# Log decay of a gated linear attention summed by a DVE scan instead of a TensorE matmul, and the heads' squares halved on GpSimd before their norm

## What is computed

```python
    log_a = jax.nn.log_sigmoid((a_code @ w_alpha + b_alpha).astype(jnp.float32)) / GLA_GATE_TEMP
...
        b = jnp.cumsum(ai, axis=2)                                  # (B,H,C,dk) cumulative log decay
...
        o_inter = jnp.einsum('bhik,bhkv->bhiv', qi * jnp.exp(b), state)
...
        new_state = jnp.exp(b_last[:, :, 0, :])[..., None] * state + jnp.einsum('bhjk,bhjv->bhkv', k_dec, vi)
...
    o = rmsnorm(o.transpose(0, 2, 1, 3), gla_head_norm)             # per-head norm, (B,S,H,dv)
    o = o.reshape(B, S, GLA_VW) * jax.nn.silu(r)
```

## Time and profile before

| what | value |
|---|---|
| median of three runs | 3164.24 us (3163.45 to 3164.89) |
| the profiled execution's own time | 3164.13 us |
| its span on the slowest core (3) | 3162.3 us |
| spans of the eight cores | 3154.3 to 3162.3 us |
| mean granted TensorE clock of the cores | 0.995 to 0.997 |
| PE busy | 3101.8 us, 98% of the span |
| DVE busy | 1186.6 us, 38% |
| ACT busy | 950.2 us, 30% |
| POOL busy | 481.1 us, 15% |

### The profile page before, as it was taken

How to read it: one execution, slowest core, us unless ns; L and a number is a source line. 1 busy time by engine, 2 the same in 40 slices (tenths; PEclk the granted TensorE clock), 3 DMA queues, 4 the chain that set the end, 5 groups by cost and what they waited for, 6 DMA issues and landing times.

```text
span 3162.3 us, 43137 instructions; the slowest of 8 cores (3154.3 to 3162.3 us)
## 1 busy us (share of the span) xinstructions
PE 3101.8 (98%) x15350; PEld 1448.9 (46%) x15350; DVE 1186.6 (38%) x1880; ACT 950.2 (30%) x1637; POOL 481.1 (15%) x557
## 2 busy tenths in 40 slices
PE   6999999999999999999999999999999999999998
PEld 2444454444444454444444445444444444544443
DVE  2231743621421373551332156363232226536212
ACT  3121442521211253252121135243212114425211
POOL 0002111220200220112110112012121021112002
PEclk9999999999999999999999999999999999999999
DMA  8597444335663534334384365232548345422534
GB/s 165 87 162 120 83 81 120 59 62 95 124 122 70 99 68 94 107 67 76 65 170 76 56 107 100 48 120 54 91 92 159 64 79 93 81 67 52 93 67 104
DMA packets 56784, 292.32 MB, mean 92 GB/s; under 512 B 5632, under 2 KB 11136, under 8 KB 32256
## 3 DMA queue, kind: packets, MB, share of 16 engines
q0 software_dynamic: 39024, 251.35, 44.5%
q1 hardware_dynamic: 17552, 38.21, 3.7%
HBM read 495.78 MB, written 22.02 MB: 164 GB/s over the span
## 4 chain that ended last, share of the span: by engine, by line
PE 94%; DVE 2%; DMA 2%; issue 1%; ACT 0%; SPq 0%; DVEq 0%; ACTq 0%; POOLq 0%; POOL 0%
PE psum_all L106 94%; DMA vo_s<-ov_mst 1%; PE psum_all L122 1%; DVE sb_hT L418 1%; DMA sb_small<-small 0%; DVE ov_nmx L1019 0%; DMA sb_slot<-ffn_w 0%; SPq L134 0%; DVE ov_Pm L1031 0%; DVE ov_pwA L733 0%; ACT ov_rstd L412 0%; DVE sb_xT L418 0%; ACT ov_rstd L410 0%; DVE ov_kT L700 0%; DVE ov_pwB L733 0%
## 5 line engine op out<-in xcount | busy, mean ns | idle before, releaser
L106 PE MATMUL psum_all<-sb_hT,sb_slot 128*128 128x512 bf16 x7680 | 1692.4, 380 | 9.0 <-DVE sb_hT L418 7.9
L106 PEld LDWEIGHTS psum_all<-sb_hT,sb_slot 128*128 128x128 bf16 x7680 | 749.8, 98 | 911.6 <-issue 23.9
L106 PE MATMUL psum_all<-ov_gated,sb_slot 128*128 128x512 bf16 x2816 | 613.2, 380 | 3.4 <-DMA sb_slot<-ffn_w 3.4
L518 DVE TENSOR_TENSOR ov_gated<-psum_all,ov_sl 128x512 bf16<-128x512 f32 x352 | 243.4, 692 | 924.0 <-PE psum_all L106 892.9
L515 ACT ACTIVATE ov_sl<-psum_all 128x512 bf16<-128x512 f32 x352 | 210.2, 597 | 902.8 <-PE psum_all L106 870.4
L106 PEld LDWEIGHTS psum_all<-ov_gated,sb_slot 128*128 128x128 bf16 x2816 | 276.0, 98 | 337.1 <-issue 6.1
L387 ACT ACTIVATE ov_sqt<-sb_xT 128x512 bf16<-128x512 f32 x224 | 140.1, 629 | 550.7 <-DVE sb_xT L539 215.8
L394 POOL TENSOR_TENSOR ov_acc<-ov_acc,ov_sqt 128x512 f32<-128x512 f32 x180 | 211.4, 1175 | 482.9 <-ACT ov_sqt L387 480.3
L134 POOL DMA_DIRECT2D sb_slot<-ffn_w x176 | 95.1, 542 | 1238.5 <-PE psum_all L106 1213.6
L106 PE MATMUL psum_all<-sb_slot,sb_hT 128*128 128x512 bf16 x1024 | 235.4, 379 | 2.6 <-DVE ov_kT L700 2.6
L418 DVE SCALAR_TENSOR_TENSOR sb_hT<-sb_xT,sb_small,ov_rstd 128x512 bf16<-128x512 f32 x192 | 141.7, 798 | 29.6 <-ACT ov_rstd L412 29.6
(11 more groups left out here) (138 smaller groups left out, 2007.7 us busy)
## 6 DMA issues: line engine op xcount, KB each, us to landing
sb_slot<-ffn_w POOLq DMA_DIRECT2D x88, 1024.0 KB, 11.2
sb_slot<-ffn_w POOLq DMA_DIRECT2D x88, 704.0 KB, 7.2
sb_slot<-w_in POOLq DMA_DIRECT2D x40, 1024.0 KB, 13.2
out<-sb_xT SPq DMA_DIRECT2D x14, 1024.0 KB, 11.9
ov_xin<-x SPq DMA_DIRECT2D x12, 1024.0 KB, 13.7
sb_slot<-w_up_a POOLq DMA_DIRECT2D x8, 1024.0 KB, 12.5
sb_slot<-w_mix_out POOLq DMA_DIRECT2D x8, 1024.0 KB, 11.2
sb_slot<-kq_s POOLq DMA_DIRECT2D x8, 1024.0 KB, 5.1
```

The costliest lines, as they stand in the source:

```text
L106: ("ins", (lambda e, o=o, l=l, r=r, st=st, sp=sp: e.matmul(o, l, r, start=st, stop=sp)), i == n - 1)
L518: S.op("dve", lambda e, b3=b3, slt=slt, j=j, s=s: e.tensor_tensor(out=gated[:, j, sl(s)], in0=b3[:], in1=slt[:], op=ALU.mult), [bb3, slb[0 ...
```

## The change

`A1` swaps the operands of its matmul, so that channels come out on partitions and tokens along the free dimension (four matmuls of 128 columns instead of one of 512), and its Ln is written back into `zb` in f32. The triangle matmul of `A2` goes; a DVE scan with multiply and add takes its place, 512 elements long, with a mask `segm` that is 0 at each head's first token. It writes `cum`, from which ACT makes `eb` and `enb`. `A2` is split: the scan and the two exponentials stand at the front of the step, ahead of `A1`, and the two multiplications (`A2b`) stand where `A2` stood. A GpSimd addition behind `osq` makes `osm`, the sum of a head's two halves, so `B_norm` needs one matmul instead of two, and `B_norm` stands behind the first filler of the step instead of at its front.

```diff
+    segm = sb("segm", [128, 4, 128], BF16)
...
-    lp2 = [ov(f"lp{i}", 75 + i, [128, 512], BF16) for i in range(2)]
+    cum, cum_b = ov("cum", 75, [128, 512], F32)
...
+    osm, osm_b = ov("osm", 99, [128, 4, 128], BF16)
...
+    S.op("dve", lambda e: e.memset(segm[:], 1.0), [], [cb2])
+    S.op("dve", lambda e: e.memset(segm[:, :, 0:1], 0.0), [], [cb2])
     S.op("dve", lambda e: e.memset(onesD[:], 1.0 / 1024.0), [], [cb2])
...
-            S.mm([(bz[:], aT[:, c * 128:(c + 1) * 128], walpha[:], True, True)], [aT_b[c // 4], wa_b], [bzb])
+            S.mm([(bz[:, h * 128:(h + 1) * 128], walpha[:, h * 128:(h + 1) * 128], aT[:, c * 128:(c + 1) * 128], True, True)
+                  for h in range(4)], [aT_b[c // 4], wa_b], [bzb])
             S.op("act", lambda e: e.activation(out=zb[:], in_=bz[:], func=AF.Exp, scale=-1.0), [bzb], zb_b)
-            S.op("act", lambda e: e.activation(out=lp[:], in_=zb[:], func=AF.Ln, bias=1.0), zb_b, lp_b)
+            S.op("act", lambda e: e.activation(out=zb[:], in_=zb[:], func=AF.Ln, bias=1.0), [], zb_b)
 
         def A2(c):
...
-            bc, bcb = psum()
-            S.mm([(bc[:, h * 128:(h + 1) * 128], lp[:, h * 128:(h + 1) * 128], triB[:], True, True) for h in range(4)],
-                 lp_b + CB, [bcb])
-            S.op("act", lambda e: e.activation(out=eb[:], in_=v4(bc[:]), func=AF.Exp, scale=-1.0 / 16.0), [bcb], eb_b)
-            S.op("act", lambda e: e.activation(out=enb[:], in_=v4(bc[:]), func=AF.Exp, scale=1.0 / 16.0), [bcb], enb_b)
+            S.op("dve", lambda e: e.tensor_tensor_scan(
+                out=cum[:], data0=segm[:].rearrange("p a b -> p (a b)"), data1=zb[:], initial=0.0,
+                op0=ALU.mult, op1=ALU.add), zb_b + CB, cum_b)
+            S.op("act", lambda e: e.activation(out=eb[:], in_=v4(cum[:]), func=AF.Exp, scale=-1.0 / 16.0), cum_b, eb_b)
+            S.op("act", lambda e: e.activation(out=enb[:], in_=v4(cum[:]), func=AF.Exp, scale=1.0 / 16.0), cum_b, enb_b)
+
+        def A2b(c):
...
             S.op("act", lambda e: e.activation(out=osq[:], in_=ov_, func=AF.Square), bank_b[0:2], osq_b)
+            oq = osq[:].rearrange("p (h v) i -> p h v i", v=2)
+            S.op("pool", lambda e: e.tensor_tensor(out=osm[:], in0=oq[:, :, 0, :], in1=oq[:, :, 1, :], op=ALU.add),
+                 osq_b, osm_b)
...
-            oq = osq[:].rearrange("p (h v) i -> p h v i", v=2)
-            S.mm([(v4(bn[:]), onesV[:], oq[:, :, vc, :], vc == 0, vc == 1) for vc in range(2)], osq_b + CB, [bnb])
+            S.mm([(v4(bn[:]), onesV[:], osm[:], True, True)], osm_b + CB, [bnb])
...
         for i in range(12):
             heavy = 3 <= i <= 8
-            if 0 <= i - 4 < 8:
-                B_norm(i - 4)
+            if 0 <= i - 1 < 8:
+                A2(i - 1)
             if i < 8:
                 A1(i)
             fill()
+            if 0 <= i - 4 < 8:
+                B_norm(i - 4)
             if 0 <= i - 1 < 8:
-                A2(i - 1)
+                A2b(i - 1)
             fill()
```

More of the change, by code:

```diff
@@ L769, in A1 @@
             zb, zb_b = zb2[c % 2]
-            lp, lp_b = lp2[c % 2]
             bz, bzb = psum()
-            S.mm([(bz[:], aT[:, c * 128:(c + 1) * 128], walpha[:], True, True)], [aT_b[c // 4], wa_b], [bzb])
+            S.mm([(bz[:, h * 128:(h + 1) * 128], walpha[:, h * 128:(h + 1) * 128], aT[:, c * 128:(c + 1) * 128], True, True)
+                  for h in range(4)], [aT_b[c // 4], wa_b], [bzb])
             S.op("act", lambda e: e.activation(out=zb[:], in_=bz[:], func=AF.Exp, scale=-1.0), [bzb], zb_b)
-            S.op("act", lambda e: e.activation(out=lp[:], in_=zb[:], func=AF.Ln, bias=1.0), zb_b, lp_b)
+            S.op("act", lambda e: e.activation(out=zb[:], in_=zb[:], func=AF.Ln, bias=1.0), [], zb_b)
         def A2(c):
-            lp, lp_b = lp2[c % 2]
+            zb, zb_b = zb2[c % 2]
             eb, eb_b = eb2[c % 2]
@@ L780, in A2 @@
             tk = slice(c * 128, (c + 1) * 128)
-            bc, bcb = psum()
-            S.mm([(bc[:, h * 128:(h + 1) * 128], lp[:, h * 128:(h + 1) * 128], triB[:], True, True) for h in range(4)],
-                 lp_b + CB, [bcb])
-            S.op("act", lambda e: e.activation(out=eb[:], in_=v4(bc[:]), func=AF.Exp, scale=-1.0 / 16.0), [bcb], eb_b)
-            S.op("act", lambda e: e.activation(out=enb[:], in_=v4(bc[:]), func=AF.Exp, scale=1.0 / 16.0), [bcb], enb_b)
+            S.op("dve", lambda e: e.tensor_tensor_scan(
[4 more added lines that the diff above has]
+        def A2b(c):
+            eb, eb_b = eb2[c % 2]
+            enb, enb_b = enb2[c % 2]
+            tk = slice(c * 128, (c + 1) * 128)
             S.op("dve", lambda e: e.tensor_tensor(out=qT[:, :, tk], in0=qT[:, :, tk], in1=eb[:], op=ALU.mult),
```

## The result

The changed kernel is slower: 3294.6 us against 3164.9, a ratio of 1.0408 (95% interval 1.0392 to 1.0425), so 130 us more. The prediction said 3289, in a range of 3240 to 3325.

What follows compares the result with a forecast made beforehand. PE, busy 98%, bounds the kernel before; after the change a step becomes DVE's and ACT's. Per tile 11.5 + 13.6 + 6.0 = 31.1 us, four 124.4; 3164.1 + 124.4 + 0.6 = 3289 us, range 3240 to 3325.

Steps and rivals of the forecast that it cites:

- What the prediction said would show: Scan about 1.2 us, 2.5 beside `Sbf`; DVE idle 4.2; scan to scan 12.9; PE waits some 30 us a tile.
- What is taken off PE: Triangle's four matmuls and one norm matmul go: 0.43 us a chunk, 32 chunks, 13.8 us gained if PE stayed the bound.
- The scan's price: DVE scan of 512 elements taken at 1.2 us, 0.7 kept for the range.
- The order: Seven ACT instructions stand between DVE's scan and its norm multiplications; DVE stands still 4.2 us for them.
- The meeting with `Sbf`: Scan on DVE meets GpSimd's state copy and is stretched: 1.3 us charged, 0 as the other bound.
- (a): Steps 1 to 4: four scans and DVE's waits make PE late, +11.5 us a tile.
- The clock: Lower granted clock behind PE's pauses, 31 us more if uncovered, 3320; part of the heavier rival, chance 0.15.
- the ring: DVE's scan, ACT's instructions, DVE's norm and followers, then the next scan: 12.9 us a step against PE's 9.1.
- (b): Steps 5 to 8: four rings of 12.9 us are 51.6, before 38.0; +13.6 us a tile.
- (c): Steps 9 to 11: no scan, but late addition and norm lie open, +2.5, +2.6 and +0.9, +6.0 us a tile.
- The mask's memset: Once at the start, it stands ahead of the constants the first matmul waits for: 0.6 us.
- The rival on the other side: PE stays the bound because other work covers DVE's stand between scan and norm: 3151 us, chance 0.09.

Runs made afterwards that it cites:

- l_scanalone: Kernel before with only `A1`'s operands swapped and the scan where the triangle matmul stood, no GpSimd addition, norm at the front: 3198.3 to 3199.7 us, ratio 1.012.
- g_cheap: Changed kernel with the scan replaced in its place by an ordinary two-input DVE multiplication: 3281.3 and 3282.7 us, ratio 1.037.
- c_expslate: Changed kernel with ACT's two exponentials moved behind the norm's two instructions: 3252.8 and 3256.7 us, ratio 1.029; the ring left over GpSimd 11.9 to 12.1 us.
- d_tri: Changed kernel with the triangle matmul back instead of the scan, new order and GpSimd addition kept: 3214.7 and 3217.7 us, ratio 1.017.
- j_sbfnext: Changed kernel with GpSimd's state copy `Sbf` issued in the next step, behind the copy of `eb`'s last column: 3257.2 and 3257.8 us, ratio 1.030.
- e_sbflate: Changed kernel with ACT's exponentials behind the norm's instructions and `Sbf` behind the GpSimd addition: 3194.3 to 3199.1 us, ratio 1.010.
- b_noosm: Changed kernel with the GpSimd addition undone, the norm having two matmuls again, order kept: 3283.0 and 3283.7 us, ratio 1.038.

## Why the prediction was right, and where it was off

**What the prediction said would show** did. Outside the four recurrences nothing moved: from the first merge matmul of one tile to the first code matmul (`sb_wa`) of the next it is 641.2 to 641.5 us, before 641.2 to 641.7. PE's waits in a recurrence are 25 to 28 us a tile, where some 30 were foretold and 0.9 stood before.

**What is taken off PE** was right in count: 64 matmuls fewer, at 0.217 us each 13.8 us, and none of it seen in the time.

**The scan's price.** Taken 1.2, with 0.7 as the other bound: 1.22, and 1.21 in all 32 of l_scanalone. The half throughput that the Trainium skill (DVE: opcode table, instruction layouts, handler registers and perf-mode slots, section Datapath and trigger behaviour) gives the scan agrees with the trace: 0.68 for the two-input multiplication in the same place (g_cheap), 1.21 for the scan, 1.8 times as long. That the scan costs as much as the reduction over 1,024 came out as assumed; no run shows that it does so for the reason given.

**The order.** Seven ACT instructions between scan and norm, 4.2 us: 4.24 to 4.37 in steps 4 to 7. That the order on ACT makes this wait is shown by c_expslate, which gives 40 of the 130 us back. It is not the whole loss: without the scan the new order and the addition still lose 52 (d_tri).

**The meeting with `Sbf`.** Charged 1.3: 2.52 - 1.22 = 1.30, and j_sbfnext takes it away. The Trainium skill (SBUF — State Buffer, section SBUF: two separate sides) has one instruction hold the shared ports as a whole. The trace agrees here as well: the scan ends 1.1 us behind `Sbf`, nearly its own length of 1.22. That GpSimd's addition is stretched by the scan in turn (2.06 for 1.15) was not in my sum; it costs nothing beside the longer ring, but is in c_expslate's 12.1.

**(a) Steps 1 to 4: the term that was mis-sized**, 11.5 a tile. From the code's matmuls to the start of step 5, PE took 1144.23 - 1111.84 = 32.4 us before and 1193.33 - 1146.45 = 46.9 after: 14.5. The rows that bound the stretches, before and after:

```profile
1111.84 0.61 PE L106 MATMUL psum_all<-sb_hT,sb_wa 128*32 128x512 bf16 x8
1214.38 1.89 PE L106 MATMUL psum_all<-ov_ogT,sb_slot 128*128 128x512 bf16 x8
...
1146.45 0.62 PE L106 MATMUL psum_all<-sb_hT,sb_wa 128*32 128x512 bf16 x8
1193.33 0.39 PE L106 MATMUL psum_all<-ov_aT,sb_walpha 128*128 128x128 bf16 x4
1243.07 3.62 PE L106 MATMUL psum_all<-sb_hT,sb_slot 128*128 128x512 bf16 x16
1281.24 1.89 PE L106 MATMUL psum_all<-ov_ogT,sb_slot 128*128 128x512 bf16 x8
```

DVE, whose rows the sum had followed, shows what the missing 3.0 us are:

```profile
1157.36 0.69 DVE L589 TENSOR_SCALAR ov_vtok<-psum_all 128x512 bf16<-128x512 f32 x1 [0.92 <-ACT ov_vtok L587]
...
1177.05 0.69 DVE L704 CAST ov_kT<-psum_all 128x512 bf16<-128x512 f32 x1 [3.23 <-PE psum_all L106]
...
1193.67 0.69 DVE L589 TENSOR_SCALAR ov_vtok<-psum_all 128x512 bf16<-128x512 f32 x1 [1.03 <-PE psum_all L106]
```

In step 1, DVE's v eviction waits 0.92 us for ACT's, because both write the same buffer mark, and ACT's is behind `eb`. The key eviction behind the banks comes 3.23 us late, where the sum had 2.6. And ahead of step 5's scan DVE waits 1.03 us for PE. The rest, 0.4 us, is in the scans and in the waits for `eb` and `rsn`. The 1.03 us comes from PE's lower clock behind its second long pause:

```profile
1163.28 5.89 PE L106 MATMUL psum_all<-sb_hT,sb_slot 128*128 128x512 bf16 x16 [4.41 <-ACT ov_zb L777]
...
1184.63 0.38 PE L106 MATMUL psum_all<-ov_vtok,ov_kg 128*128 128x256 bf16 x2 [3.77 <-ACT ov_zb L777]
...
1186.33 3.57 PE L106 MATMUL psum_all<-sb_slot,sb_hT 128*128 128x512 bf16 x8
```

Behind the first pause, 4.41 us and not 3.3, 16 matmuls took 5.89 us instead of 3.62 at a granted clock of 0.60, and by the rows it cost nothing: neither DVE nor ACT waited for them, and PE itself then waited again for `zb`. The clock was one of my rivals, at 31 us if nothing covered it. It fell as that rival said, but most of what it took is inside the ring's slack; e_sbflate and l_scanalone, where PE has little slack, paid more of it.

**(b) Steps 5 to 8**, 13.6 a tile: 51.5 us (1193.33 to 1244.80) against 38.0, 13.5. The number is right, and partly by luck. From scan to scan it is 12.0, 13.0 and 13.2 us, and only the last two of these are the ring of 12.9 that I had computed. The first is 12.0 us, because the scan, late by those 1.03, met only the end of `Sbf` (1.54 for 1.22). In step 8 there is no `A1`, which my four equal rings overlooked: five ACT instructions stand between scan and norm, and DVE is idle for 3.16 us instead of 4.24. What fills the gap is the clock: PE's matmuls at 1236.15 took 3.57 us instead of 1.89, so step 9 began 1.7 us later.

**(c) Steps 9 to 11**, 6.0 a tile: from there (1244.80, the second half of the 16 matmuls at 1243.07) to the first merge matmul 36.4 us after (to 1281.24) and 32.2 before (to 1214.38): 4.3. Too high by 1.7; in step 9 PE came to the norm 1.7 us late, so it waited 0.24 us for the addition and not 2.0. What is missing in (c) stands in (b). The tile's sum is 32.3 where I had 31.1. (a) was too small by 3.0, (b) and (c) together too large by 1.8, and that these nearly cancel is luck. The mask's memset, put at 0.6 us, held up the first constants by 0.9.

**The rival on the other side**, that PE stays the bound, wanted the idle time between scan and norm under 2 us. It is 4.2.

## What to carry to other kernels

Before an instruction is moved to the front of a step, write down for each queue what stands right behind it, and what *that* waits for: an early producer whose consumers stand ahead of unrelated work on a second engine makes two in-order queues wait for each other, and a ring of 13 us grows where DVE is busy for two thirds of the time, ACT for under half, and over the whole span both for about a third. Moving two instructions on ACT was worth 40 us here, halving the price of the scan 12 to 15. And when work is taken from the engine that bounds, look at what the receiving engine has left in the tightest steps, not on average.

## What the runs showed of the hardware that I had not expected

- A DVE instruction with two SBUF inputs and a GpSimd instruction stretch each other both ways: a DVE scan of 1.22 us took up to 2.87 beside GpSimd's copy (b_noosm), and a GpSimd addition of 1.15 took 2.06 beside the scan.
- The granted clock fell behind shorter pauses of PE than the 3.39 us of the earlier trace rows, and not always. Behind pauses of 2.56 us in two successive steps, eight matmuls took 1.89 us the first time, at a granted clock of 1.00, and 3.16 the second, at 0.59. Longer ones were no surer: behind 3.49 us they took 1.89 in e_sbflate, behind 3.50 us 3.37 in l_scanalone (rows above). So the length of the pause just before does not decide it alone. The two pauses of 2.56 us:

```profile
1210.01 0.38 PE L106 MATMUL psum_all<-ov_osm,sb_onesV 128*128 128x512 bf16 x1 [2.56 <-POOL sb_ebl L799]
1210.23 1.89 PE L106 MATMUL psum_all<-sb_slot,sb_hT 128*128 128x512 bf16 x8
...
1223.01 0.59 PE L106 MATMUL psum_all<-ov_osm,sb_onesV 128*128 128x512 bf16 x1 [2.56 <-POOL sb_ebl L799]
1223.39 3.16 PE L106 MATMUL psum_all<-sb_slot,sb_hT 128*128 128x512 bf16 x8
```
